# Squares of the second token half of both MLPs summed by TensorE in four column groups; last output tiles moved ahead of most of the other half's split

## The reference, cut to what matters

```python
def first_block(x, ...):
    ...
    h = rmsnorm(x, norm_mlp_pre)
    m = square(relu(h @ w_ff1)) @ w_ff2          # 1024 -> 4096 -> 1024
    x = x + rmsnorm(m, norm_mlp_post)
    return x
def second_block(x, ...):
    ...
    hx = modulate(rmsnorm(x, pre_mix_g), sh1, sc1)
    ...
    hm = modulate(rmsnorm(x, pre_mlp_g), sh2, sc2)
    x = x + g2 * rmsnorm(square(relu(hm @ w_mlp1)) @ w_mlp2, post_mlp_g)
    return x
def rmsnorm(x, g):
    return x * rsqrt(mean(x * x, axis=-1) + EPS) * g
```

## Time and profile before

| what | value |
|---|---|
| median of 3 executions | 2876.25 us (2870.07, 2876.25, 2879.12) |
| the profiled execution, its own time | 2878.11 us |
| its span (first to last recorded instruction) | 2876.3 us |
| busy TensorE, VectorE, ScalarE, GpSimd | 94%, 58%, 21%, 34% |
| mean granted TensorE clock | 0.974 of full |

### The profile page before, as it was taken

One profiled execution on the slowest core, in us unless ns is written; L12 is line 12 of the kernel. 1 busy time (PEld: TensorE's weight loads), 2 busy tenths in 40 slices (PEclk: granted clock), 3 DMA queues, 4 the chain that ended last, 5 costly groups with the idle time before them and its releaser, 6 DMA issues. The chain is left out here.

```text
span 2876.3 us, 32497 instructions
## 1 busy us (share of the span) xinstructions
PE 2716.8 (94%) x12492; PEld 2183.4 (76%) x12492; DVE 1662.8 (58%) x2225; ACT 609.6 (21%) x901; POOL 982.0 (34%) x515
## 2 busy tenths in 40 slices
PE   7899999999999999977988999989989999999997
PEld 5688877778888888856776776568767888888885
DVE  8877545756556565675646985963375222222247
ACT  4232232310110011132332103732121110001111
POOL 2122215553333333441112332013545333333343
PEclk9899999999999999987999999999999999999998
DMA  3111142223323222231001333341322111111123
GB/s 137 36 53 43 51 139 81 96 81 103 95 80 95 95 95 92 91 103 57 29 29 37 103 118 118 108 169 48 114 95 81 52 51 44 51 44 51 44 73 102
DMA packets 88484, 228.88 MB, mean 80 GB/s; under 512 B 27520, under 2 KB 30720, under 8 KB 88384
## 3 DMA queue, kind: packets, MB, share of 16 engines
q1 hardware_dynamic: 52384, 172.81, 18.4%
q10 hardware_dynamic: 36000, 54.69, 6.2%
HBM read 197.98 MB, written 28.31 MB: 79 GB/s over the span
## 5 line engine op out<-in xcount | busy, mean ns | idle before, releaser
L195 POOL CAST w_hi<-w_raw 128x1024 fp32r<-128x1024 f32 x254 | 282.7, 1113 | 1829.6 <-PE ps L208 1818.5
L204 PE MATMUL ps<-a_hi,w_hi 128*128 128x512 f32 x2080 | 690.7, 400 | 44.9 <-POOL w_lo L197 18.4
L197 POOL TENSOR_TENSOR w_lo<-w_raw,w_hi 128x1024 fp32r<-128x1024 f32 x254 | 696.4, 2742 | 20.3
L206 PE MATMUL ps<-a_lo,w_hi 128*128 128x512 f32 x2080 | 674.8, 393 | 0.0
L208 PE MATMUL ps<-a_hi,w_lo 128*128 128x512 f32 x2080 | 672.4, 391 | 0.0
L204 PEld LDWEIGHTS ps<-a_hi,w_hi 128*128 128x128 f32 x2080 | 389.8, 190 | 137.4 <-issue 32.6
L206 PEld LDWEIGHTS ps<-a_lo,w_hi 128*128 128x128 f32 x2080 | 394.6, 190 | 83.4
L208 PEld LDWEIGHTS ps<-a_hi,w_lo 128*128 128x128 f32 x2080 | 393.2, 189 | 84.4
L206 PE MATMUL ps<-g_b,w_hi 128*128 128x512 f32 x1216 | 421.0, 397 | 0.0
L204 PE MATMUL ps<-g_b,w_hi 128*128 128x512 f32 x1088 | 370.5, 397 | 9.9 <-DVE g_b L1765 9.9
L208 PE MATMUL ps<-g_b,w_lo 128*128 128x512 f32 x1088 | 368.8, 396 | 0.0
(11 more groups left out here) (453 smaller groups left out, 2776.7 us busy)
## 6 DMA issues: line engine op xcount, KB each, us to landing
w_raw<-in_wstream SPq DMA_DIRECT2D x254, 512.0 KB, 3.5
ada_w<-in_ada_w ACTq DMA_DIRECT2D x25, 512.0 KB, 3.5
ada_w_m<-in_ada_w ACTq DMA_DIRECT2D x25, 512.0 KB, 3.4
y_by_token<-y ACTq DMA_DIRECT2D x12, 512.0 KB, 4.3
x_res_b<-in_xT SPq DMA_DIRECT2D x2, 2048.0 KB, 11.4
x_block<-x_res_b SPq DMA_DIRECT2D x16, 256.0 KB, 3.0
z_rows<-ada_w ACTq DMA_DIRECT2D x8, 512.0 KB, 2.6
u_rows<-pad ACTq DMA_DIRECT2D x8, 512.0 KB, 4.4
```

What stands on the lines that cost most here:

```text
L195: pool.tensor_copy(k.w_hi[:, s, :], k.w_raw[:, s, :]).then_inc(k.w_high, 1)
L197: pool.tensor_tensor(k.w_lo[:, s, :], k.w_raw[:, s, :], k.w_hi[:, s, :].bitcast(F32), ALU.subtract).then_inc(k.w_split, 1)
L204: pe.matmul(o, w_hi, a_hi[:, c], start=first, stop=False)
L206: pe.matmul(o, w_hi, a_lo[:, c], start=False, stop=False)
```

## The change

For token half 1 of both MLPs the squares are no longer added by DVE. `wide_sums_pe` lets PE sum each squared tile as it comes, two squares behind each output tile, into bank 2 in four column groups; `wide_out_act` lets ACT copy the bank to `acc`, and `fold_pe` does the four one-column products with `fold_col`. The signal `added` now comes from PE, so ACT's squares wait for PE before they reuse a buffer of `tmp`. DVE takes output tiles 2 and 3 one directly behind the other, ahead of the split of half 0's tiles 3 to 7; `inverse_dve` of half 1 moves in between the split of tiles 3 to 5 and that of 6 and 7. On ACT, the last two squares, the copy and the root of half 1 move ahead of half 0's high parts 3 to 7.

```diff
--- before.py
+++ after.py
@@ -1045,13 +1045,13 @@
         self.k, self.w, self.gain, self.following = k, w, gain, following
         self.x_loaded = ctx.enter_context(nc.semaphore(f"{name}_x_loaded")) if loads else None
         s = signals(nc, ctx, name, "sq added sums root inv row scaled x_new sq_new summed root_new inv_new row_new "
-                                   "raw hi lo parted part_out")
+                                   "raw hi lo parted part_out sq_out")
         self.sq, self.added, self.sums, self.root, self.inv, self.row = (
             s[n] for n in ("sq", "added", "sums", "root", "inv", "row"))
         self.scaled, self.x_new, self.sq_new, self.summed = (s[n] for n in ("scaled", "x_new", "sq_new", "summed"))
         self.root_new, self.inv_new, self.row_new = (s[n] for n in ("root_new", "inv_new", "row_new"))
         self.raw, self.hi, self.lo = (s[n] for n in ("raw", "hi", "lo"))
-        self.parted, self.part_out = s["parted"], s["part_out"]
+        self.parted, self.part_out, self.sq_out = s["parted"], s["part_out"], s["sq_out"]
 
     def sums_pe(self, pe, h):
         k, w = self.k, self.w
@@ -1060,6 +1060,27 @@
             at = (h * HC + c) * P
             ins = pe.matmul(k.ps[:, 4 + h, c:c + 1], w.acc[:, at:at + P], k.mean_col[:, :], start=True, stop=True)
         ins.then_inc(self.sums, 1)
+
+    def wide_sums_pe(self, pe, ts):
+        k, w = self.k, self.w
+        for t in ts:
+            g = t % GROUPS_PE
+            pe.wait_ge(self.sq, KT + t + 1)
+            pe.matmul(k.ps[32 * g:32 * (g + 1), 2, :], k.mean_col[:, :].broadcast_to([P, 32]), w.tmp[:, t % 2, half_of(1)],
+                      start=t < GROUPS_PE, stop=t >= KT - GROUPS_PE).then_inc(self.added, 1)
+
+    def fold_pe(self, pe):
+        k, w = self.k, self.w
+        pe.wait_ge(self.sq_out, 1)
+        for c in range(HC):
+            at = (HC + c) * P
+            ins = pe.matmul(k.ps[:, 5, c:c + 1], w.acc[:, at:at + P], k.fold_col[:, :], start=True, stop=True)
+        ins.then_inc(self.sums, 1)
+
+    def wide_out_act(self, act):
+        k, w = self.k, self.w
+        act.wait_ge(self.added, 2 * KT)
+        act.activation(w.acc[:, half_of(1)], k.ps[:, 2, :], ACT.Copy).then_inc(self.sq_out, 1)
 
     def spread_pe(self, pe, h):
         k, w = self.k, self.w
@@ -1601,6 +1622,8 @@
                     other.sums_new_pe(pe, 1 - h, range(KT // 2, KT))
                 if other and other.following and t == 1:
                     other.row_new_pe(pe, 1 - h)
+                if not first and h == 1 and t:
+                    other.wide_sums_pe(pe, range(2 * t - 2, 2 * t))
 
         half_step(True, 0, before)
         half_step(True, 1, None)
@@ -1622,7 +1645,8 @@
         steady(pe, step)
         half_step(False, 0, None)
         half_step(False, 1, turn)
-        turn.sums_pe(pe, 1)
+        turn.wide_sums_pe(pe, range(KT - 2, KT))
+        turn.fold_pe(pe)
         turn.row_pe(pe, 1)
         if turn.following:
             turn.tail_sums_pe(pe, 1)
@@ -1706,10 +1730,15 @@
             if own:
                 squares(2)
             if other and other.following:
-                for t in range(2, KT):
-                    other.high_act(act, t, o)
+                other.high_act(act, 2, o)
             if own:
                 squares(3)
+            if own and h == 1:
+                own.wide_out_act(act)
+                own.root_act(act, 1)
+            if other and other.following:
+                for t in range(3, KT):
+                    other.high_act(act, t, o)
 
         if ada:
             for m in range(2):
@@ -1738,7 +1767,6 @@
         if ada:
             for m in range(2):
                 act.wait_ge(ada_in[m], (ADA_TILES // 2 + 1) * 16)
-        turn.root_act(act, 1)
         if turn.following:
             for t in range(KT):
                 turn.square_new_act(act, t, 1)
@@ -1806,21 +1834,26 @@
             take(0)
             if other and other.following:
                 other.inverse_new_dve(dve, o)
-            if own:
+            sums = own and h == 0
+            if sums:
                 add(0)
             take(1)
             if other and other.following:
                 other.split_dve(dve, range(0, 3), o)
-            if own:
+            if sums:
                 add(1)
             take(2)
-            if other and other.following:
-                other.split_dve(dve, range(3, KT), o)
-            if own:
+            if sums:
                 add(2)
             take(3)
-            if own:
+            if sums:
                 add(3)
+            if other and other.following:
+                other.split_dve(dve, range(3, 6), o)
+            if own and h == 1:
+                own.inverse_dve(dve, 1)
+            if other and other.following:
+                other.split_dve(dve, range(6, KT), o)
 
         half_step(True, 0, before, None)
         half_step(True, 1, None, None)
@@ -1865,7 +1898,6 @@
             modulations(dve, k, ch, False)
         half_step(False, 0, None, turn)
         half_step(False, 1, turn, turn)
-        turn.inverse_dve(dve, 1)
         turn.residual_dve(dve, range(KT), 1)
         if turn.following:
             turn.inverse_new_dve(dve, 1)
```

## The result

The changed kernel took 2884.80 us (median of 14 executions, 2881.15 to 2889.07) against 2875.73 us (14 executions of the kernel before, 2870.07 to 2879.12). The ratio is 1.0037, 95% interval 1.0029 to 1.0044, so 8 to 13 us slower. The forecast was 2878.7 us, a change too small to be told from none. What is missing in it is the cost at a place that the prediction never looked at.

The account below looks back on a forecast made before the run. TensorE, busy 94% of the span, was taken as the bound. Second MLP +3.25 us and first MLP -0.8 gave +2.4 us, on a median of 2876.25 making 2878.7 us; range 2871 to 2886 us.

Parts of the forecast that it names:

- What bounds the kernel: Whole kernel: TensorE, busy 94% of the span; a VectorE addition (58% busy) matters only where TensorE stands still.
- The change touches two such places: Claim that the change touches two places where TensorE stands still, the ends of the two MLPs.
- the reordering does nothing: Second MLP: no norm follows, so only the sums change and the new order costs nothing.
- A pair at 1.08 us: Both MLPs: each pair of column-group products costs TensorE 1.08 us (0.96 to 1.52); two pairs delay the last output product 2.16.
- Behind T, second MLP: After TensorE's last output product there, one-column products start 4.05 us later instead of 2.96, costing 1.09; with pairs +3.25.
- bound (c): Low-end case: a full clock for longer shortens the last spread from 1.11 to 0.6 us, -0.5.
- First MLP's end: Sums come 5.4 us earlier, but the residual only moves from 1293.27 to 1292.45: gain 0.8 us.
- the wait for the high part: First MLP's end: VectorE's low part 3 waits for ScalarE's high part behind the root; reciprocal delayed, 2.9 us of gain lost.
- The clock: After each MLP's last output product, TensorE's clock was taken as full as far as the one-column products.
- bound (b): Clock falling at once after the last output product: each MLP costs 1.8 us more.
- rival 1: Clock falls right behind the last output product in both MLPs and pairs cost 1.52: +8.7 us, 2885; chance 0.14.
- Rivals 2 and 3: First MLP: full clock through its tail, -1.2 us, 2875, chance 0.08; whole 5.4 us gained, -3.0 us, 2873, chance 0.06.

Follow-up runs that it names:

- experiment 2: The kernel before, with only the first steps of both MLPs reordered: VectorE takes output tile 3 ahead of splitting tiles 3 to 7; 2883.31 us, ratio 1.0032.
- Experiment 4: experiment 3 with the first MLP's last-step split spread over VectorE's idle time and ScalarE's high parts reordered; 2884.78 us, ratio 1.0026.
- experiment 1: The changed kernel with the first half steps' old order restored: VectorE splits tiles 3 to 7 ahead of taking tile 3; 2874.19 us, ratio 1.0005.
- experiment 7: The changed kernel with the old VectorE and ScalarE order in all steps, so only the sums on TensorE remain; 2878.58 us, ratio 1.0012.
- experiment 8: experiment 1 with VectorE adding the squares again, so only the last step's new order remains; 2888.24 us, ratio 1.0047.
- experiment 6: Experiment 4 plus four unread VectorE additions, 2.5 us of delay, behind the first MLP's last split; 2872.18 us, ratio 0.9999.
- experiment 3: experiment 1 with the second MLP's squares added by VectorE again, so TensorE column-group sums remain in the first MLP only; 2874.42 us, ratio 1.0001.

## Why the prediction was wrong, point by point

- **What bounds the kernel** was read rightly for the two ends, wrongly by "The change touches two such places". It touches four. `half_step` is called with a following norm in the first step of each MLP too, where `own` is absent but `other` is not, and the diff reorders `other.split_dve` there. The sentence on the second MLP, "the reordering does nothing", was the same mistake. In the first steps the taken tile 3 is in nobody's way and the split is what TensorE needs next, so the early take is pure loss: 7.3 us by the traces of the changed kernel and the kernel before, 5.7 to 12.6 by experiment 2. This is the step that failed: a path that the change makes longer stood in the sum at nothing, without a reason.
- **A pair at 1.08 us**: nearly right, and well inside its bounds. A pair costs as much as four products, not half; but it is 1.18 us, since the second step behind it is slow as well, by 0.10.
- **Behind T, second MLP**: 4.00 against 4.05 forecast for the one-column products. The spread took 0.65, not 1.11, which was bound (c); so the end cost 2.9 us in place of 3.25.
- **First MLP's end**: root at T+5.10 (5.2 forecast), reciprocal 3.01 behind the root's start (3.2), residual at T+11.95 (12.3), gain 1.15 (0.8). The wait for the high part is there with its row, at half the length. Experiment 4 shows that the wait and the standing split were worth 4.3 us.
- **The clock** stayed full as far as the one-column products at both ends, as taken; bound (b) was not used. It fell where I had not looked, in the first steps.
- **The rivals**: rival 1 had the right sign and nearly the right size (+8.7) for a cause that did not occur; 1.05 in both places rules it out. Rivals 2 and 3 did not occur; the sums over the new squares took the same 13.81 us.
- **The sum**: +2.4 forecast for the ends, +1.8 in the traces, +1.4 (-1.1 to +4.0) in experiment 1. The missing term was +7.3 by the traces, 9.2 by the middle of experiment 2.
- **What can be told**: the forecast took 0.3%, 8.6 us, for the least difference that shows. With 14 executions of each kernel the interval is 0.15% wide, so a difference of 0.37% stands clear of it. That 2884.8 us still lies inside 2871 to 2886 is luck: the upper end was made of rival 1 and the spread of executions, and neither is what happened.

## What to carry to other kernels

When a diff edits a helper, list every call of it with its arguments before costing anything, and cost each branch that the edit changes in each call; here one helper served four places with opposite needs. In each, ask who needs the moved work next: at an end the sums were urgent and the split was not, at a start it was the other way. A wide sum on TensorE costs where TensorE is the bound and VectorE idle, as at the end of the second MLP (2.9 us). It came out about even where VectorE's queue was the bound (experiment 7, first MLP); that it pays anywhere is shown by no run here.

## What the runs showed of the hardware that was not expected

- A stall of 2.82 us inside a tile cost more than its own length: the granted clock fell to 0.56 and 0.58 over the next two stretches of 4 us, so the tile (12.6 us from its first product to ScalarE's next activation, against 7.9 before) lost 4.7 us. In the kernel before, a stall of 1.14 us at that place left the clock at 1.00.
- The untouched middle of the kernel has two levels some 15 us apart, which TensorE's mean clock over the span tells apart: 0.968 to 0.971 on the upper level in experiments 4 and 8, 0.975 to 0.977 in their four other executions. The kernel before was never on the upper one in 83 executions beside these experiments; experiments 4 and 8 were in 19 of 23, and a delay of 2.5 us ahead of the middle brought them down again. Their first MLPs ended 5.8 and 2.2 us earlier, but experiment 6, 3.0 us earlier, was on the upper level only once in twelve, so the shift alone does not say which level comes. Nor does the time since the start of the execution: by the first cast of the middle, the traces of experiments 4 and 8 lie 6.8 and 6.6 us ahead of the kernel before, those of experiments 1 and 3 lie 4.0 and 3.8 us ahead on the lower level, and that of experiment 7 lies 3.4 us ahead on the upper level. It is shown for two kernels that the added work ahead of the middle brings the level down, and that on the kernel before it costs its own length within the interval. Whether it acts by the later start or by something else in the added instructions was not separated, and the rule is open.
- VectorE's addition with both inputs in SBUF took 2.72 us beside GpSimd's 2.35 us subtraction and 0.69 otherwise (experiment 8); the takes, with one input in PSUM, kept 0.67 and 0.68 beside such a subtraction of 2.74 us.
